# A network block on one core: the first stage rebuilt around row sums of squares, and four opening orders changed

## The chip, the cores and the metric

The kernel runs on one core of one Trainium2 chip. The metric is the device time of one execution in microseconds (us). Engines are named as the profile names them: PE (TensorE), DVE (VectorE), ACT (ScalarE), POOL (GpSimd) and SP (SyncE, which here only issues transfers).

## What is computed

All arrays are float32; the width D and the sequence are 1024, a context of 256 rows is read beside it. A block of two layers is followed by a pooling mixer and a convolutional FFN (hidden width 2816). Cut to what matters here:

```python
def rms_norm(x, g):
    y = x * lax.rsqrt(jnp.mean(x * x, axis=-1, keepdims=True) + EPS)
    return y * g

for i in range(2):
    shift, scale, gate = jnp.split(jax.nn.silu(c) @ ada_w[i] + ada_b[i], 3, axis=-1)   # and for c_ctx
    h = rms_norm(x, norm_g[i]) * (1.0 + scale) + shift
    if i == 0:
        lam = exp(sum(lambda_q1 * lambda_k1)) - exp(sum(lambda_q2 * lambda_k2)) + lam_init
        hc = rms_norm(ctx, norm_g[0]) * (1.0 + scale_c) + shift_c
        # proj = h @ w_in; k, v also of hc; differential attention with lam, a Fourier mix,
        # a silu gate, and the product with even_w_out
    else:
        bg, cg, xt, g = jnp.split(h @ odd_w_in, 4, axis=-1)
        u = cg * xt
        y = (bg * conv3(u, conv_w) * jax.nn.silu(g)) @ odd_w_out
    x = x + gate * y
x = x + pool_mixer(rms_norm(x, norm_mix_g))
val, gate = jnp.split(causal_conv3(rms_norm(x, norm_ffn_g) @ ffn_w_in, conv_w, conv_b), 2, axis=-1)
x = x + (jax.nn.silu(gate) * val) @ ffn_w_out
```

## The kernel before

The program is a row of blocks of code. In each block every engine runs its own list of instructions in the order in which it is written, and counters (semaphores) join them; nothing reorders. Most products are made in three passes of TensorE on operands that are split into a high and a low part (hi with hi, lo with hi, hi with lo): ACT makes the high part (`split_high`, L127), DVE or POOL the low part (`split_low`, L130). A tile has 128 partitions; D is eight tiles (`KT`), the sequence eight blocks of rows (`RT`), the context two (`CT`).

**First block**, `adaptive_parameters` (from L325). SP issues, in this order: the identity, x in two halves (2 MB each), 12 sets of small rows (biases, gains, the vectors c and c_ctx, taps) into `rows`, the four lambda vectors, the context (1 MB), and eight tiles of `ada_w` (1 MB each, `ada_raw`), then four slices of `even_w_in` (256 KB each). PE turns the small rows into columns (L388), turns x tile by tile into two pairs of PSUM banks (L398), makes ada products 0 to 2 (L299), turns the context (L416), and goes on with products 3 to 7, between which stand the column sums of the squares (L210, products with `ones`) and the spreads (L218, which turn a column of reciprocal roots into full rows). ACT copies each turned tile of x into `fq` (L447) and squares the tile before it (L154); DVE adds the squares up (L173). The context's squares are one instruction on ACT (L458) and one reduction on DVE (L488). Then come root, reciprocal, spread and the copies `rstd_x`, `rstd_c` (L183). When the last product is done, DVE copies its sum (`ada_rows`, L495), PE turns it (L307) and DVE makes shift and gain columns (L314, L320).

**Projections**, `even_projections` (from L560). For tile k of h, DVE multiplies x with gain and reciprocal root into `scaled` (L191, buffer `gate`), ACT adds the shift and rounds (`h_hi`, L165), DVE makes the rest (`h_lo`, L202). The class `Norm` holds these steps. PE (L685) starts tile k of the first unit (named k) when `h_lo` of tile k stands; a unit's slice of weights is split by ACT and POOL into `in_hi` and `in_lo`, in a ring of four.

**Conv stage**, `conv_layer` (from L1419) and **FFN**: both make products by a scheme of seven products for each group g, in the order p1, p6, p2, p5, p7, p3, p4 (`UP`). p1 and p2 use one bank, so p2 of group g waits for `p1_copy(g)` (L1758 in the conv stage, L2753 in the FFN) on ACT; p4 waits for c22, one of the sums that DVE makes out of finished banks (L1885, L2887). The first two groups are made without the scheme, and are copied out by `plain_out` (L1800, L2803). In the conv stage `gated_input` (DVE, L1908) makes u, `middle_tap` (ACT, L1768) the middle tap of the convolution, `tap_before` and `tap_after` (DVE, L1912, L1917) the others; `differences(kk)` (L1965) makes and splits operands of the seven products. In the FFN `ga_tap2` (ACT, L2780) and `ga_taps` (DVE, L2906, L2909) are the same for the gate half. N is the number of FFN groups; the products with `ffn_w_out` (L3090) follow in closing steps t, whose operands `high_pair` (ACT) and `low_s`, `low_t` (DVE, POOL) split into `down_ring`.

## Time and profile before

| | |
|---|---|
| median of 3 runs | 1856.58 us (1854.06 to 1858.5) |
| the profiled execution | 1857.68 us, its span 1855.9 us |
| mean granted TensorE clock | 0.985 of full |
| PE busy | 1774.3 us, 96% |
| DVE, ACT, POOL busy | 1167.8, 800.6, 757.2 us |
| moved by DMA | 188.31 MB, mean 101 GB/s |

A busy PE means that its matmuls follow each other, not that they run at full clock; the granted clock is listed apart, as a fraction of 2.4 GHz. Idle time of an engine that nobody waits for costs nothing. The time of one execution is its span and 1.8 us around it. The view of waits names for each wait what ended it; a bracket behind a row of the timeline says how long the engine had been idle before that row and who released it. A row of the timeline with a count stands for instructions that follow each other.

### The profile page before, as it was taken

The numbers are of one execution on the slowest core, as the hardware profiler recorded it, in microseconds if no ns is written. First come the engines' busy times: TensorE is split into PE (matmuls) and PEld (weight loads), VectorE is DVE, ScalarE is ACT, GpSimd is POOL, SyncE is SP. The second block draws the span as 40 slices with busy tenths as digits, with TensorE's granted clock in tenths as the row PEclk, the third lists the DMA queues.
The fourth block names the chain that finished last, engine by engine and source line by source line (L and its number), as shares of the span: only waits on it lengthen the run. The fifth ranks groups of instructions, "written<-read, shape, count | busy, mean of one in ns | idle before, by whom it ended". The sixth has DMA issues, their size and how long they took to land.

```text
span 1855.9 us, 22927 instructions
## 1 busy us (share of the span) xinstructions
PE 1774.3 (96%) x8745; PEld 1474.4 (79%) x8745; DVE 1167.8 (63%) x1315; ACT 800.6 (43%) x1244; POOL 757.2 (41%) x452
## 2 busy tenths in 40 slices
PE   5899999899999799999999999999999999999999
PEld 3688888668888688878888888987888888878887
DVE  3703876338888832965454653497666666779876
ACT  5324221346666632643333442655444444444443
POOL 0325322000000123356666531257999999920000
PEclk9899999899999999999999999999999999999999
DMA  8414113460000180212221341312232223187333
GB/s 324 149 48 117 46 46 102 177 245 1 0 0 0 46 268 32 65 57 79 69 80 57 118 155 46 94 43 73 76 91 80 91 80 91 57 310 262 138 120 124
DMA packets 162089, 188.31 MB, mean 101 GB/s; under 512 B 9231, under 2 KB 117320, under 8 KB 160840
## 3 DMA queue, kind: packets, MB, share of 16 engines
q1 hardware_dynamic: 161991, 187.00, 30.6%
q8 instruction: 64, 1.05, 0.2%
q14 instruction: 34, 0.27, 0.1%
HBM read 152.37 MB, written 34.60 MB: 101 GB/s over the span
## 4 chain that ended last, share of the span: by engine, by line
PE 50%; DVE 5%; ACT 2%; issue 2%; DMA 1%; POOL 0%; SPq 0%; ACTq 0%; DVEq 0%; POOLq 0%
PE ps L3039 18%; PE ps L2043 14%; PE ps L3090 10%; PE ps L2103 5%; PE ps L3390 1%; PE ps L3052 1%; DMA y_a<-y_scratch 1%; DVE cv_lo_p L130 1%; DVE up_lo_p L130 1%; DVE residual L2906 0%; DVE residual L1965 0%; ACT residual L3226 0%; DMA res_scratch<-x_nat 0%; PE ps L3056 0%; DVE residual L2945 0%
## 5 line engine op out<-in xcount | busy, mean ns | idle before, releaser
L3039 PE MATMUL ps<-up_hi_p,st_hi_p 128*128 128x512 f32 x560 | 218.0, 389 | 3.6 <-issue 2.0
L3039 PE MATMUL ps<-up_lo_p,st_hi_p 128*128 128x512 f32 x560 | 217.9, 389 | 0.0
L3039 PE MATMUL ps<-up_hi_p,st_lo_p 128*128 128x512 f32 x560 | 217.8, 389 | 0.0
L3090 PE MATMUL ps<-down_ring 128*128 128x512 f32 x924 | 210.7, 389 | 2.1 <-DVE down_ring L130 1.9
L3090 PEld LDWEIGHTS ps<-down_ring 128*128 128x128 f32 x924 | 173.2, 188 | 39.4 <-DVE down_ring L130 2.7
L130 POOL TENSOR_TENSOR in_lo<-in_raw,in_hi 128x512 fp32r<-128x512 f32 (+1 forms) x56 | 92.4, 1659 | 233.0 <-ACT in_hi L127 182.6
L2043 PE MATMUL ps<-cv_hi_p,cv_st_hi_p 128*128 128x512 f32 x392 | 153.4, 391 | 4.5 <-issue 4.5
L2043 PE MATMUL ps<-cv_lo_p,cv_st_hi_p 128*128 128x512 f32 x392 | 153.0, 390 | 0.0
L2043 PE MATMUL ps<-cv_hi_p,cv_st_lo_p 128*128 128x512 f32 x392 | 153.0, 390 | 0.0
L130 POOL TENSOR_TENSOR st_lo_p<-up_raw,st_hi_p 128x512 fp32r<-128x512 f32 x68 | 100.9, 1487 | 67.2 <-ACT st_hi_p L127 67.2
L3039 PEld LDWEIGHTS ps<-up_hi_p,st_hi_p 128*128 128x128 f32 x560 | 105.1, 188 | 26.2 <-issue 2.4
L1885 DVE TENSOR_TENSOR residual<-ps,residual 128x512 f32<-128x512 f32 x70 | 48.3, 691 | 120.4 <-PE ps L2043 120.4
L3039 PEld LDWEIGHTS ps<-up_hi_p,st_lo_p 128*128 128x128 f32 x560 | 105.1, 188 | 21.9
L3039 PEld LDWEIGHTS ps<-up_lo_p,st_hi_p 128*128 128x128 f32 x560 | 105.1, 188 | 21.6
L685 PE MATMUL ps<-in_hi,h_hi 128*128 128x512 f32 x256 | 100.8, 394 | 7.3 <-DVE h_lo L202 6.9
L1243 ACT ACTIVATE prob<-ps,neg_peak 128x1280 f32<-128x1280 f32 x64 | 84.9, 1327 | 48.2 <-DVE neg_peak L1337 48.2
L2887 DVE TENSOR_TENSOR residual<-ps,residual 128x512 f32<-128x512 f32 x100 | 68.0, 685 | 58.6 <-PE ps L3039 58.1
L1337 DVE TENSOR_REDUCE neg_peak<-ps 128x1 f32<-128x1280 f32 x64 | 95.2, 1487 | 11.4 <-PE ps L1149 11.3
L1149 PE MATMUL ps<-k_turned,q_turned 128*128 128x512 f32 (+1 forms) x384 | 91.7, 375 | 10.7 <-ACT prob L1243 4.6
L685 PE MATMUL ps<-in_lo,h_hi 128*128 128x512 f32 x256 | 100.6, 393 | 0.0
L685 PE MATMUL ps<-in_hi,h_lo 128*128 128x512 f32 x256 | 100.5, 392 | 0.0
L130 POOL TENSOR_TENSOR cv_st_lo_p<-cv_raw,cv_st_hi_p 128x512 fp32r<-128x512 f32 x50 | 74.7, 1502 | 52.1 <-ACT cv_st_hi_p L127 52.1
(377 smaller groups left out, 4209.0 us busy)
## 6 DMA issues: line engine op xcount, KB each, us to landing
up_raw<-in_ffn_w_in SPq DMA_DIRECT2D x44, 512.0 KB, 5.2
w_raw<-in_ffn_w_out SPq DMA_DIRECT2D x66, 256.0 KB, 3.0
ada_raw_rest<-in_ada_w SPq DMA_DIRECT2D x32, 512.0 KB, 6.1
cv_raw<-in_odd_w_in SPq DMA_DIRECT2D x32, 512.0 KB, 5.4
in_raw<-in_even_w_in SPq DMA_DIRECT2D x48, 256.0 KB, 2.8
y_scratch<-residual SPq DMA_DIRECT2D x22, 512.0 KB, 2.6
ada_raw<-in_ada_w SPq DMA_DIRECT2D x8, 1024.0 KB, 17.3
residual<-in_x SPq DMA_DIRECT2D x2, 2048.0 KB, 10.3
```

The source lines that it names most:

```text
L130: return eng.tensor_tensor(dst, src, high.bitcast(F32), ALU.subtract).then_inc(done, 1)
L685: last = pe.matmul(ps[:, bank, :], x[:, k, r * P:(r + 1) * P], w[:, n % RING, :], start=(k == 0 and x is x_hi and w is in_hi), stop=(k == ...
L1149: last = pe.matmul(score[m][:, b:e], q_turned[:, m, t * P:(t + 1) * P], k_turned[:, m, part, b:e], start=(part == 0), stop=(part == 1))
L1243: act.activation(prob[:, t % 2, m, :], score[m], ACT.Exp, bias=neg_peak[:, t, m:m + 1], accum_out=total[:, t, m:m + 1]).then_inc(sem("expe ...
L1337: dve.tensor_reduce(neg_peak[:, t, m:m + 1], score[m], AX_X, ALU.max, negate=True)\
L1885: dve.tensor_tensor(dst, ps[:, bank(g, p), :], base, ALU.add).then_inc(sem(name), 1)
L2043: last = pe.matmul(out, w[a_], x[b_], start=(first and a_ == 0 and b_ == 0), stop=(stop and a_ == 1), skip_group_check=skip)
L2103: last = pe.matmul(ps[:, 2 * (d % 4) + c, :], w[a_], x[k][:, c * BANK:(c + 1) * BANK], start=(k == 0 and a_ == 0 and x is y_hi), stop=(k = ...
L2887: dve.tensor_tensor(dst, ps[:, bank(j, p), :], base, ALU.add).then_inc(sem(name), 1)
L3039: last = pe.matmul(ps[:, bank(j, p), :], w[p][:, kk * P:(kk + 1) * P], x[p][:, kk, :], start=(first and w is st_hi and x is up_hi), stop=( ...
L3052: pe.matmul(ps[:, plain_bank(j, kind, side), :], part[FIRST_SLOT[j][kind, half]][:, ks], x_hi, start=(kk == 0 and half == 0 and part is st ...
L3090: last = pe.matmul(ps[:, 4 * (i % 2) + m, :], slot[:, s, m * P:(m + 1) * P], slot[:, x, :], start=(k == 0 and s == 0 and x == 2 and DOWN[i ...
```

## The change

Five things are edited.

1. The squares are summed along the natural rows of x and of the context: ACT squares a block of rows with a sum along the row into one column of `compact`. The squares of the turned tiles, their additions, the reduction of the context's squares and the products with `ones` are gone. DVE instead of ACT copies the turned tiles of x. PE spreads x's reciprocal roots behind ada product 1, the context's behind product 4.
2. The order of transfers: identity, x, the first 7 sets of small rows, ada 0 to 3, the context, ada 4 and 5, the other 6 sets, ada 6, weight slice 0, ada 7, slices 1 to 3. Column tile 0 is turned first, tiles 1 and 2 behind ada product 5. POOL splits slice 0 inside the first block.
3. Lambda is computed in the projections: its four loads stand behind the spills of x, its exponential on ACT ahead of the first root.
4. The first tile of h is made in halves of 512 columns; PE starts behind the left one. POOL waits for the first tile before it splits slices 1 to 3, and ACT's splits of these stand behind the first tile.
5. Four opening orders: conv stage, ACT `p1_copy(2)` behind `middle_tap(0)`; conv stage, DVE `gated_input(0)` behind `differences(3)`; FFN, ACT `ga_tap2(0)` ahead of `p1_copy(2)`; end of the FFN, ACT `ga_tap2(N - 1)` and `silu(N - 1)` each one `high_pair` earlier, DVE `ga_taps(N - 1)` ahead of `low_t(4)`, and `low_s(5)`, `low_t(5)` behind `product(N - 1)`.

```diff
--- the first block, transfers
-                        for t, r, src in row_sources:
+                        for t, r, src in row_sources[:FIRST_ROWS]:
                             sp.dma_start(rows[r:r + src.shape[0], t, :], src).then_inc(sem("rows_in"), 16)
-                        for n, name in enumerate(("even_lambda_q1", "even_lambda_k1", "even_lambda_q2", "even_lambda_k2")):
-                            sp.dma_start(lam_in[:, n, :], a[name].broadcast_to([P, DH])).then_inc(sem("lam_in"), 16)
-                        sp.dma_start(nat[:, RT:KEYT, :], ctx_rows).then_inc(sem("ctx_in"), 16)
                         for k in range(KT):
+                            if k == 4:
+                                sp.dma_start(nat[:, RT:KEYT, :], ctx_rows).then_inc(sem("ctx_in"), 16)
+                            if k == 6:
+                                for t, r, src in row_sources[FIRST_ROWS:]:
+                                    sp.dma_start(rows[r:r + src.shape[0], t, :], src).then_inc(sem("rows_late"), 16)
+                            if k == KT - 1:
+                                load_slice(sp, 0)
                             sp.dma_start(ada_raw[:, k, :], a["ada_w"][0, k * P:(k + 1) * P, 0:len(ADA_FIRST) * BANK])\
                               .then_inc(sem(f"ada_in{k}"), 16)
...
--- the first block, ACT
+                            act.activation(square[:, r % 2, :], nat[:, r, :], ACT.Square, accum_out=compact[:, r:r + 1])\
+                               .then_inc(sem(done), 1)
...
-                        for k in range(KT):
-                            act.wait_ge(sem("xt_turned"), k + 1)
-                            act.activation(x_t[:, k, :], pair[k % 2], ACT.Copy).then_inc(sem("xt_copied"), 1)
-                            if k:
-                                act.wait_ge(sem("xt_copied"), k)
-                                stats.scalar_square(act, k - 1)
+                        rooted(compact[:, 0:RT], "in_x_squared", RT, "in_x_rooted")
+                        act.wait_ge(sem("ctx_in"), 16)
+                        for r in range(RT, KEYT):
+                            squared(r, "c_squared")
+                        rooted(compact[:, RT:KEYT], "c_squared", CT, "c_rooted")
...
--- the first block, DVE
+                        for k in range(KT):
+                            dve.wait_ge(sem("xt_turned"), k + 1)
+                            dve.tensor_copy(x_t[:, k, :], pair[k % 2]).then_inc(sem("xt_copied"), 1)
...
--- the projections, first tile on DVE
+            def vector_first_halves(self, dve):
+
+                self.scale(dve, 0, LEFT, "scaled_left")
+                self.scale(dve, 0, RIGHT, "scaled")
+                dve.wait_ge(self.s("high_left"), 1)
+                self.lower(dve, 0, LEFT, "low_left")
+                dve.wait_ge(self.s("high"), 1)
+                self.lower(dve, 0, RIGHT, "low")
...
--- the projections, ACT
-                        for n in range(1, RING):
-                            high_slice(act, n)
                         for k in range(KT):
-                            norm_x.scalar_high(act, k)
+                            if k == 0:
+                                norm_x.scalar_high_left(act)
+                            norm_x.scalar_high(act, k, RIGHT if k == 0 else None)
+                            if k == 0:
+                                for n in range(1, RING):
+                                    high_slice(act, n)
...
--- the conv stage, ACT
-                p1_copy(2)
                 for kind, side in PLAIN_OUT:
                     plain_out(1, kind, side)
                 for p in ("p3", "p4"):
                     high_stationary(act, p, 2)
-                moving_stands(act, "p4", HALF - 1)
                 middle_tap(0)
                 for g in range(2, G - 1):
-                    if g > 2:
-                        p1_copy(g)
+                    p1_copy(g)
...
--- the conv stage, DVE
+                differences(3)
                 gated_input(0)
-                differences(3)
...
--- the FFN, ACT
+                ga_tap2(0)
                 p1_copy(2)
-                ga_tap2(0)
...
--- the end of the FFN, DVE
+                ga_taps(N - 1)
                 low_t(dve, SLOTS)
-                low_s(dve, LOW_FIRST)
-                low_t(dve, LOW_FIRST)
-                ga_taps(N - 1)
                 product(N - 1)
```

The first block on PE before, from the turns of the small rows (L388) to the turn of the last sum (L307); L299 is an ada product, L210 a sum of squares, L218 a spread, L416 a turn of the context:

```order
1 L388 MATMUL ps<-ident,rows 128x120
2 L388 MATMUL ps<-ident,rows 128x104
3 L388 MATMUL ps<-ident,rows 128x89
4 L398 MATMUL ps<-ident,residual 128x128 x64
5 L299 MATMUL ps<-ada_raw,cond 32x512 x12
6 L416 MATMUL ps<-ident,residual 128x128 x16
7 L299 MATMUL ps<-ada_raw,cond 32x512 x12
8 L210 MATMUL ps<-ones,square_sum 128x1 x8
9 L299 MATMUL ps<-ada_raw,cond 32x512 x4
10 L210 MATMUL ps<-ones,square_sum_c 128x1 x2
11 L218 MATMUL ps<-ident,compact 128x128 x8
12 L299 MATMUL ps<-ada_raw,cond 32x512 x4
```

The same place on PE now (L283 is the ada product, L374 a spread, L405 a turn of the context):

```order
1 L367 MATMUL ps<-ident,rows 128x120
2 L393 MATMUL ps<-ident,residual 128x128 x64
3 L283 MATMUL ps<-ada_raw,cond 32x512 x8
4 L374 MATMUL ps<-ident,compact 128x128 x8
5 L283 MATMUL ps<-ada_raw,cond 32x512 x8
6 L405 MATMUL ps<-ident,residual 128x128 x16
7 L283 MATMUL ps<-ada_raw,cond 32x512 x4
8 L374 MATMUL ps<-ident,compact 128x128 x2
9 L283 MATMUL ps<-ada_raw,cond 32x512 x4
10 L367 MATMUL ps<-ident,rows 128x104
11 L367 MATMUL ps<-ident,rows 128x89
12 L283 MATMUL ps<-ada_raw,cond 32x512 x8
```

The sums with `ones` are gone, both spreads stand ahead of product 5, and the context's turns moved from behind product 2 to behind product 3.

The opening of the conv stage on ACT before; L1758 is `p1_copy(2)`, L1800 `plain_out(1)`, L1768 `middle_tap(0)`, L1776 `silu`, L1762 the copy of c11:

```order
275 L1758 ACTIVATE residual<-ps 128x512
276 L1800 ACTIVATE residual<-ps 128x512 x4
277 L127 ACTIVATE cv_st_hi_p<-cv_odd_sums 128x512
278 L127 ACTIVATE cv_st_hi_p<-cv_raw 128x512
279 L1768 ACTIVATE residual<-residual,cols 128x1024
280 L127 ACTIVATE cv_st_hi_p<-cv_raw 128x512
```

And now (L1818 `plain_out(1)`, L1786 `middle_tap(0)`, L1776 `p1_copy(2)`):

```order
265 L1818 ACTIVATE residual<-ps 128x512 x4
266 L128 ACTIVATE cv_st_hi_p<-cv_odd_sums 128x512
267 L128 ACTIVATE cv_st_hi_p<-cv_raw 128x512
268 L1786 ACTIVATE residual<-residual,cols 128x1024
269 L1776 ACTIVATE residual<-ps 128x512
270 L128 ACTIVATE cv_st_hi_p<-cv_raw 128x512
```

The copy that p2 of group 2 waits for moved from ahead of seven instructions to behind them.

## Rows read from the trace of the kernel before

**Rows 1.** The page, part 1: busy time, share and instructions of PE.

```profile
PE 1774.3 (96%) x8745; PEld 1474.4 (79%) x8745; DVE 1167.8 (63%) x1315; ACT 800.6 (43%) x1244; POOL 757.2 (41%) x452
```

**Rows 2.** PE's waits from 12 to 60 us: total us, times, longest.

```profile
PE ps L388 <- DMA rows<-in_even_subln: 16.8, 1, 16.8
```

**Rows 3.** Busy time by stretch: start:end, length, PE, PEld, DVE, ACT, POOL, clock, DMA, GB/s.

```profile
14.40:18.10 3.70, 1.32 (x7) 1.33 (x8) 0.50 (x3) 0.00 (x0) 0.00 (x0) 1.00 0.16 40
22.00:32.00 10.00, 6.93 (x60) 4.87 (x62) 4.90 (x4) 10.00 (x12) 0.00 (x0) 1.00 1.01 424
```

**Rows 4.** The tile ada_raw: its eight loads' issues, and issue to landing.

```profile
L378 SPq DMA_DIRECT2D ada_raw<-in_ada_w x8: 432/600/3479, 11.1 to 18.4; - x8
...
DMA to landing us min/median/max: 13.0/17.3/24.0
```

**Rows 5.** Timeline, first block: start, us, engine, line, operation; bracket: idle before, releaser.

```profile
24.83 1.03 ACT L447 ACTIVATE fq<-ps 128x1024 f32<-128x1024 f32 x1
25.73 1.07 ACT L154 ACTIVATE gate<-fq 128x1024 f32<-128x1024 f32 x1
...
46.50 1.07 PE L299 MATMUL ps<-ada_raw,cond 128*32 128x512 f32 x8
...
46.60 1.78 DVE L183 COPY residual<-ps 128x1024 f32<-128x1024 f32 x2 [0.47 <-PE ps L218]
48.30 0.68 DVE L495 COPY ada_rows<-ps 128x512 f32<-128x512 f32 x1
```

**Rows 6.** Timeline, start of the projections.

```profile
50.72 3.49 DVE L191 SCALAR_TENSOR_TENSOR gate<-fq,mod_gain,residual 128x1024 f32<-128x1024 f32 x2 [0.32 <-PEq L366]
50.77 9.01 POOL L130 TENSOR_TENSOR in_lo<-in_raw,in_hi 128x512 fp32r<-128x512 f32 x4 [50.32 <-POOLq L366]
...
54.13 2.29 DVE L202 SCALAR_TENSOR_TENSOR h_lo<-gate,ada_col,h_hi 128x1024 fp32r<-128x1024 f32 x1
...
56.57 0.76 PE L685 MATMUL ps<-in_hi,h_hi 128*128 128x512 f32 x1 [6.87 <-DVE h_lo L202]
...
62.10 1.28 DVE L202 SCALAR_TENSOR_TENSOR h_lo<-gate,ada_col,h_hi 128x1024 fp32r<-128x1024 f32 x1
```

**Rows 7.** Stretches with a granted clock of 0.50; columns as in rows 3.

```profile
37.78:41.20 3.42, 3.42 (x17) 0.78 (x21) 1.92 (x2) 3.40 (x3) 0.00 (x0) 0.50 0.99 405
51.40:61.70 10.30, 5.13 (x12) 4.09 (x13) 10.23 (x6) 4.28 (x5) 8.38 (x4) 0.50 0.32 94
809.20:812.60 3.40, 3.17 (x8) 2.53 (x9) 0.72 (x2) 0.29 (x1) 3.40 (x4) 0.50 0.38 154
```

**Rows 8.** Timeline by engine, opening of the conv stage (DVE, ACT, PE).

```profile
788.57 2.31 DVE L1908 TENSOR_TENSOR residual<-residual 128x1024 f32<-128x1024 f32 x1
...
797.74 2.12 DVE L1912 SCALAR_TENSOR_TENSOR residual<-residual,cols 128x1023 f32<-128x1023 f32 x1 [3.66 <-ACT residual L1768]
...
793.10 0.58 ACT L1758 ACTIVATE residual<-ps 128x512 f32<-128x512 f32 x1
...
796.53 1.18 ACT L1768 ACTIVATE residual<-residual,cols 128x1024 f32<-128x1024 f32 x1
...
793.88 0.41 PE L2043 MATMUL ps<-cv_hi_p,cv_st_hi_p 128*128 128x512 f32 x1
...
809.42 0.77 PE L2043 MATMUL ps<-cv_hi_p,cv_st_hi_p 128*128 128x512 f32 x1 [4.48 <-issue]
```

**Rows 9.** Timeline by engine, opening of the FFN (ACT, PE).

```profile
1261.83 1.25 ACT L2780 ACTIVATE residual<-residual,cols 128x1024 f32<-128x1024 f32 x1 [3.06 <-DVE up_lo_p L130]
...
1273.62 0.47 PE L3039 MATMUL ps<-up_hi_p,st_hi_p 128*128 128x512 f32 x1 [2.05 <-issue]
...
1283.56 0.47 PE L3039 MATMUL ps<-up_hi_p,st_hi_p 128*128 128x512 f32 x1 [1.53 <-ACT residual L2753]
```

**Rows 10.** Timeline of DVE, closing products of the FFN.

```profile
1649.96 1.27 DVE L2906 SCALAR_TENSOR_TENSOR residual<-residual,cols 128x1023 f32<-128x1023 f32 x1
...
1664.78 0.69 DVE L2565 TENSOR_TENSOR y_a<-y_a 128x512 f32<-128x512 f32 x1 [1.45 <-DMA y_a<-y_scratch]
```

More of the change, by code:

```diff
@@ L199, in vector_scale @@
                             dve.wait_ge(self.s("low"), k)
-                        scale(k + 1)
+                        self.scale(dve, k + 1, whole, "scaled")
                     dve.wait_ge(self.s("high"), k + 1)
-                    dve.scalar_tensor_tensor(out=self.low(k), in0=self.scaled[:, k % 2, 0:self.n], scalar=self.shift(k),
-                                             in1=self.high(k).bitcast(F32), op0=ALU.add, op1=ALU.subtract)\
-                       .then_inc(self.s("low"), 1)
-            def tensor_mean(self, pe, sums):
-                pe.wait_ge(self.s("summed"), sums)
-                for r in range(self.n // P):
-                    last = pe.matmul(self.mean[:, r:r + 1], self.total[:, r * P:(r + 1) * P], ones[:, 0:1],
-                                     start=True, stop=True)
-                last.then_inc(self.s("meaned"), 1)
+                    self.lower(dve, k, whole, "low")
             def tensor_spread(self, pe, parts=1):
@@ L401, in _ @@
                         pe.wait_ge(sem("cond_ready"), 1)
-                        def ada(first, end):
-                            for k in range(first, end):
-                                pe.wait_ge(sem(f"ada_in{k}"), 16)
-                                last = ada_product(pe, ADA_FIRST, 6, k, cond,
-                                                   [ada_raw[:, k, i * BANK:(i + 1) * BANK] for i in range(len(ADA_FIRST))])
-                            return last
-                        ada(0, 3)
+                        ada(0, 2)
+                        spread(spread_x, range(RT), "in_x_inverse").then_inc(sem("in_x_spread"), 1)
+                        ada(2, 4)
                         pe.wait_ge(sem("ctx_in"), 16)
+                        pe.wait_ge(sem("xt_copied"), KT)
                         for k in range(0, KT, 4):
@@ L671, in _ @@
                     def _(pool):
-                        for n in range(N_SLICES):
+                        pool.wait_ge(norm_x.s("low"), 1)
+                        for n in range(1, N_SLICES):
                             pool.wait_ge(sem("in_high"), n + 1)
```

224 lines of the change are left out of this document (116 added, 108 removed).

## The prediction

> **What bounds the kernel now.** I read the page first: TensorE (PE) is busy 96% of the span [rows 1], so only time in which PE stands, or runs at a low clock, can be won. Its waits come next: 16.8 us for the first loads, in the stage that the change rebuilds [rows 2]. Then the transfers: the share of the DMA engines and the GB/s say whether a stretch is bound by loading. They run full, 424 GB/s, through the middle of the first block, but from 14.4 to 18.1, where only small rows and the lambda vectors are under way, they are nearly idle [rows 3]. The last tile of `ada_raw` is issued at 18.4 and lands 24.0 us later, at 42.4 [rows 4]. The timeline of the first block shows the rest: a copy on ScalarE (ACT) with a square behind it for each turned tile of x, and after the last ada product (46.50) a row of short dependent steps [rows 5]. The projections' start is a chain on VectorE (DVE) from 50.72 to PE's 56.57, with 6.87 us of waiting on PE [rows 6]. Of TensorE's clock, three stretches show a granted 0.50, that is 1.2 instead of 2.4 GHz [rows 7]. Last, the openings of the conv stage, of the FFN and of its closing products, where PE or DVE wait 4.48, 2.05, 1.53 and 1.45 us [rows 8 to 10].
>
> **First block, from its start to E.** Call E the moment at which the projections may begin (50.72, the first DVE scale [rows 6]). Loads first. Before, the 2.48 us that one MB of `ada_raw` takes at 424 GB/s [rows 3] are paid for 4 MB of x, 1 MB of ctx and 8 MB of ada; between the end of x (14.4) and the return of the full rate (18.1) lie 3.7 us in which mostly the 16 small loads are under way [rows 3], and by the sizes of their arrays they carry some 0.3 MB. The change leaves 7 of them ahead, puts 6 behind ada5 (between large ones, which can keep the engines full), moves four (lambda) out of the block and brings slice 0 (256 KB, 0.62 us) in. If the small loads behind large ones are nearly free, the last ada tile lands about 2.1 us earlier for them (9 of 16 small loads' share of 3.7) and 0.62 later for the slice: 42.4 - 2.1 + 0.6 = 40.9.
>
> The TensorE side: x turns start when 7 instead of 12 rows have come, about 15.7 instead of 16.8. Before, each tile took a period of 1.86, which is ACT's copy of 1.03 and its square of 1.07 less overlap (24.83 and 25.73 are the starts of one pair, 0.9 apart [rows 5]). After, DVE copies alone; 128x1024 plus 128x256 took 1.78 in two copies [rows 5], so 1.2 to 1.4 for one, and eight take some 11 us instead of 15, to about 28. ACT takes the sums from natural rows meanwhile (10 squares of about 1.07, 10.7 us, starting as soon as the first half of x lies), so it is no bound. Gone from DVE are seven additions and one reduction, from PE ten small matmuls. Then PE follows the ada tiles: the last product begins at 41.1 if the clock is high, and at 43.1 if it falls at about 37 as it did at 37.78 for 3.42 us [rows 7], since an ada product of 1.07 (the eight matmuls at 46.50 [rows 5]) then takes 2.1. Before, it began at 46.50, 4.1 us after its data, because ctx copies, sums and spreads stood ahead of it in PE's order.
>
> From that product to E took 50.72 - 46.50 = 4.22, of which 0.7 were the wait of the `ada_rows` copy (48.30) for the two rstd copies (46.60 to 48.38) on DVE [rows 5]; those now lie earlier. That leaves 3.5, so E is 44.6 to 46.7; since the block still has pauses of the kind that preceded the low clock, I take 45.9: **-4.8** (bounds -3.8 and -6.0).
>
> **From E to the first matmul.** Before: two whole scales, 3.49 for the pair beside GpSimd (POOL), `h_hi` 1.1, `h_lo` 2.29, and PE starts at 56.57, E + 5.85 [rows 6]. After: the left half's scale, high, low. The price of a whole `h_lo` alone is 1.28 (at 62.10) against 2.29 while POOL works [rows 6], and POOL now waits for the first tile's low. Half of 1.28 is 0.68 with the fixed part; two halves of the scale queue before the low on DVE, ACT's half high (0.6) lies beside the second. 0.68 + 0.6 + 0.7 + some 0.2 of signals = 2.2: **-3.65** (bounds -3.0 and -4.0). What is late next? Tile 1: POOL's three splits, moved behind the first low, meet its scale, and ACT splits slices 1 to 3 (3 x 0.6) first. Its low ends at about E + 9.3; PE is through tile 0 at the low clock at E + 2.2 + 7.1 to 8.8, that is E + 9.3 to 11. No stall, with little to spare. Lambda moves into the projections, where PE has work and DVE's steps go ahead of a norm that waits for PE anyway; its result is wanted only in the attention. Without that cover its nine tiny instructions would cost under 3 us. Stage sum: **-8.45**.
>
> **Conv opening.** PE's p2(2) must wait for `p1_copy(2)` (the ACT row L1758 at 793.10 [rows 8]), which goes behind the first middle tap (L1768). The tap waits for `gated_input(0)` (DVE L1908, 2.31 at 788.57), now behind `differences(3)`. Before, p2(2) began at 793.88 [rows 8]; after, DVE makes the differences first, ACT is done with its splits and plain outputs some 1.5 us sooner, the tap starts at about 795 to 796 and the copy is done at 796.5 to 797: a new stall of 2.7 to 3.1 at p2(2). It lies under the old one: PE stood 4.48 us, until p4(2) at 809.42, because c22 came late on DVE behind the two taps that began at 797.74 [rows 8]. The taps now begin 1.0 to 1.6 us sooner, so p4(2) starts at 807.8 to 808.5: -0.9 to -1.6. The 3.40 us of low clock behind that stop [rows 7] cost 1.7. One long pause becomes a shorter one and almost none; either the clock stays (-1.7 more), or it falls at p2 and costs the same there under cover. I take **-2.0** (bounds -0.3, if the fall delays p4(2) too, and -3.0).
>
> **FFN opening.** `p1_copy(2)` goes behind `ga_tap2(0)` (L2780), which waits to 1261.83 [rows 9]. PE's four products p2, p5, p7, p3 took 809.42 - 4.48 - 793.88 = 11.06 in the conv stage [rows 8]; the same before 1273.62 - 2.05 puts p2(2) of the FFN at 1260.5. Now it starts at 1261.83 + 1.15 + 0.6 + 0.1 = 1263.7, a stall of 3.2. The pause of 2.05 before 1273.62 takes 2.05 of it, so p4(2) is 1.1 late; the pause of 1.53 before 1283.56, which waits for ACT's next copy, takes part of that. **+0.7** (0 to +2.0, the upper end with a fall of the clock).
>
> **FFN closing.** On DVE `ga_taps(N-1)` (L2906 and its twin, two of 1.27 from 1649.96 [rows 10]) moves ahead of `low_t(4)`, for which PE waits: 2.0 to 3.0 of new stall. The 1.45 for which DVE waits for a landing before 1664.78 [rows 10] may take part of it, though that load is issued later too: **+1.75** (0.9 to 2.6).
>
> **Sum.** -4.8 - 3.65 - 2.0 + 0.7 + 1.75 = -8.0. Against the profiled execution (1857.68, span 1855.9) that is 1849.7; the median of the runs (1856.58) lies 1.1 lower, by which it is 1848.6. I take **1849.0**.
>
> **The rivals.**
> Small loads cost the same wherever they stand. For it: 3.7 us for 16 of them at 32 GB/s [rows 3]. Then only the lambda loads are saved, the last tile lands at about 42.2, and with a low clock E is 47.7: 1.8 less, 1850.8.
> The Trainium skill, DMA: Bandwidth & Descriptors, section Rules for kernel authors, says of many small transfers to coalesce them, since under 64 KB one pays mostly overhead; moving them would not help by that. No row here shows small ones between large ones, so the trace does not decide it; by the rule the sum would be the 1850.8 of this rival.
> The orders cost more than said: conv gains nothing (0 for -2.0) and the FFN's clock falls (+2.0 for +0.7): -4.7, 1852.3.
> The clock stays high at the projections' start. It was low for 10.30 us from 51.40 [rows 7], behind PE's long idle; a pause of 2.2 instead of 5.9 may not bring it down: 2.5 to 3 more, 1846.2. Against it: the fall at 37.78 [rows 7] came behind much shorter pauses than the one before 56.57.
> The block is not shorter, since something unseen replaces its chain, and only the halves help: -3.2, 1853.8.
> **The slower side.** The low clock at the start lasts on. A tile is 24 matmuls, two of the products of 2.76 worked out above: 5.5 at the high clock, 11 at half of it. DVE makes a tile's operands in 4.4 us beside POOL (2 x 2.2 [rows 6]), and now PE is 3.65 us nearer to them. If PE runs into `h_lo` of tiles 1, 2, 3 and the clock therefore stays low through three tiles more, that is 3 x 5.5 less 2 that it costs already, +14, so +6 against before: 1863. It decides from where tile 1's `h_lo` comes later than the end of tile 0, at E + 9.3 to 11.
>
> **How the numbers follow.** Forecast 0.53, small loads 0.15, orders 0.12, clock high 0.12, block not shorter 0.05, slower 0.03. A measurement of this kernel tells about 0.2% (3.7 us) from no change, so faster means below 1852.9: nearly all of the forecast, of the small loads and of the high clock, and half of the orders, 0.85; the same 0.11; slower 0.04. The bounds of the terms add (as independent) to about 2.5 either way; with the high clock at 1846 and the orders at 1852.3 the range is 1845.0 to 1853.5.
>
> **What would show it.** After: the last ada product at 41 to 43.5 and E at 44.6 to 46.7; first projection matmul at E + 2.2; no PE wait at tile 1; a wait of about 3 before p2(2) in the conv stage, and at most a short one before p4(2), with p4(2) of the same products then 0.9 to 1.6 us nearer to the stage's start; a wait of 3.2 at p2(2) of the FFN and of 2 to 3 at its fourth closing step. I am wrong if the DMA rate sinks where the six rows stand, if PE waits for `h_lo` of tile 1, or if the stalls at p2(2) reappear in full at p4(2).

## The result

The changed kernel takes 1844.70 us (median of 6 runs, 1842.64 to 1848.65) where the kernel before takes 1855.62 (6 runs, 1854.04 to 1858.5). The ratio is 0.9942, with a 95% interval of 0.9929 to 0.9954: 10.9 us, or 0.6%, faster. The forecast was 1849.0 with a range of 1845.0 to 1853.5. The direction was right, and three of the five terms came out within their bounds. The first block gained more than its bounds allowed and the closing products lost less; the whole gain was larger than the range allowed, by 0.3 us.

The two profiled executions have spans of 1855.9 and 1846.2, so the traces have 9.7 us to explain. First the page of the changed kernel, its busy times and clock.

```profile
span 1846.2 us, 22891 instructions
PE 1773.9 (96%) x8725; PEld 1474.8 (80%) x8725; DVE 1167.8 (63%) x1317; ACT 798.6 (43%) x1250; POOL 762.2 (41%) x452
```

PE does the same work as in [rows 1], to 0.4 us. What went is time in which it stood. Its waits in the changed kernel, total us, times, longest:

```profile
PE ps L367 <- DMA rows<-in_c_ctx: 15.9, 1, 15.9
...
PE ps L3101 <- DVE down_ring L131: 3.7, 2, 2.1
PE ps L689 <- DVE h_lo L172: 3.5, 1, 3.5
...
PE ps L3050 <- ACT residual L2768: 2.9, 1, 2.9
...
PE ps L2058 <- ACT residual L1776: 2.7, 1, 2.7
```

The first row answers [rows 2] (16.8). The wait for `h_lo` is 3.5 where [rows 6] has 6.87. The waits of 4.48 and 2.05 at p4(2) (p4 of group 2) [rows 8, 9] are gone, and in their place stand 2.7 and 2.9 at p2(2), for `p1_copy(2)`, as the prediction said; the closing products wait 3.7 instead of 1.9.

The transfers, in the stretches of [rows 3] (length, PE, PEld, DVE, ACT, POOL, clock, DMA share, GB/s) and where they end:

```profile
14.40:18.10 3.70, 2.16 (x10) 2.16 (x11) 0.28 (x1) 3.65 (x7) 0.00 (x0) 1.00 0.99 394
22.00:32.00 10.00, 9.58 (x79) 5.67 (x78) 7.19 (x8) 2.69 (x6) 0.00 (x0) 1.00 1.03 411
...
39.00:40.00 1.00, 1.00 (x14) 0.24 (x8) 0.00 (x0) 0.00 (x0) 0.00 (x0) 0.85 0.56 209
40.00:41.00 1.00, 1.00 (x13) 0.38 (x16) 0.43 (x2) 0.00 (x0) 0.00 (x0) 1.00 0.05 18
```

The pause behind x, 40 GB/s before, is gone altogether: 394 GB/s. That is the row that the prediction had not foreseen. The last tile of `ada_raw` is issued at 21.99 and lands at 39.13, where the kernel before had 42.47 and the prediction 40.9. The timeline of the first block and of the projections' start:

```profile
35.70 1.80 PE L283 MATMUL ps<-ada_raw,cond 128*32 128x512 f32 x8 [1.11 <-ACT residual L450]
...
39.96 1.92 PE L283 MATMUL ps<-ada_raw,cond 128*32 128x512 f32 x16
...
44.38 1.41 DVE L168 SCALAR_TENSOR_TENSOR gate<-fq,mod_gain,residual 128x512 f32<-128x512 f32 x2 [0.32 <-PEq L341]
45.92 1.41 DVE L172 SCALAR_TENSOR_TENSOR h_lo<-gate,ada_col,h_hi 128x512 fp32r<-128x512 f32 x2
...
46.81 0.77 PE L689 MATMUL ps<-in_hi,h_hi 128*128 128x512 f32 x1 [3.46 <-DVE h_lo L172]
```

E, the first DVE scale, is at 44.38 (50.72 in [rows 6]), and PE starts the projections at 46.81, 2.43 behind it (5.85 before). The low clock, as in [rows 7]:

```profile
35.90:39.30 3.40, 3.40 (x18) 0.49 (x10) 0.42 (x1) 0.63 (x1) 1.27 (x1) 0.50 0.97 381
46.10:52.90 6.80, 6.08 (x14) 4.81 (x15) 6.80 (x5) 4.31 (x6) 5.49 (x3) 0.50 0.17 52
786.80:790.20 3.40, 3.40 (x10) 2.62 (x9) 3.37 (x3) 0.02 (x1) 2.19 (x2) 0.50 0.53 157
1251.00:1254.40 3.40, 3.10 (x7) 2.49 (x8) 2.34 (x3) 3.38 (x7) 1.67 (x1) 0.51 0.00 0
```

It now falls at p2(2) in both schemes (PE starts these at 786.44 and 1251.30). In the conv stage it is no longer at p4(2); in the FFN the first trace of before had none at the opening.

### The profile page after: what moved, and what is told of

The parts are those of the page before. It is cut to its first block, busy times and chain, and to the rows that moved or that the text cites. A ratio compares the mean times of both kernels' runs of the same rounds, so it can differ in the third digit from the quotient of the medians.

```text
span 1846.2 us, 22891 instructions
## 1 busy us (share of the span) xinstructions
PE 1773.9 (96%) x8725; PEld 1474.8 (80%) x8725; DVE 1167.8 (63%) x1317; ACT 798.6 (43%) x1250; POOL 762.2 (41%) x452
## 4 chain that ended last, share of the span: by engine, by line
PE 52%; DVE 4%; ACT 2%; issue 1%; DMA 1%; SPq 0%; ACTq 0%; DVEq 0%
PE ps L3050 20%; PE ps L2058 14%; PE ps L3101 10%; PE ps L2118 5%; PE ps L3401 1%; PE ps L3063 1%; DMA y_a<-y_scratch 1%; DVE cv_lo_p L131 1%; DVE up_lo_p L131 1%; DVE residual L1980 0%; ACT residual L3237 0%; PE ps L3067 0%; DVE residual L2959 0%; ACT cv_hi_p L128 0%; ACT residual L1797 0%
## 5 line engine op out<-in xcount | busy, mean ns | idle before, releaser
L131 POOL TENSOR_TENSOR in_lo<-in_raw,in_hi 128x512 fp32r<-128x512 f32 (+1 forms) x56 | 97.7, 1754 | 218.4 <-ACT in_hi L128 172.4
L1169 PE MATMUL ps<-k_turned,q_turned 128*128 128x512 f32 (+1 forms) x384 | 91.7, 375 | 10.6 <-ACT prob L1263 4.5
## 6 DMA issues: line engine op xcount, KB each, us to landing
residual<-in_x SPq DMA_DIRECT2D x2, 2048.0 KB, 10.4
```

The lines of the kernel that those rows point to most:

```text
L131: return eng.tensor_tensor(dst, src, high.bitcast(F32), ALU.subtract).then_inc(done, 1)
L1169: last = pe.matmul(score[m][:, b:e], q_turned[:, m, t * P:(t + 1) * P], k_turned[:, m, part, b:e], start=(part == 0), stop=(part == 1))
```

## Where the 9.7 us come from, and how much of it is chance

From the first projection matmul on, PE runs the same matmuls in the same order in every kernel here. So the start of one and the same matmul can be compared between two traces, and the lead of one kernel over the other be read at each place. The table has the lead over the first trace of the kernel before, in us, where that trace stands at the time in the head. It has all traces, those of the experiments too (the part that differs is named in the section of each).

| kernel | 56.57 | 330 | 370 | 790 | 812.9 | 1255 | 1500 | end |
|---|---|---|---|---|---|---|---|---|
| changed | 9.76 | 9.27 | 11.09 | 10.32 | 11.96 | 12.30 | 11.74 | 9.70 |
| changed, second trace | 10.63 | 10.56 | 13.30 | 13.65 | 14.07 | 15.55 | 15.71 | 13.97 |
| e1 old orders | 10.04 | 11.49 | 14.56 | 13.88 | 13.49 | 14.48 | 14.73 | 14.66 |
| e2 old closing | 10.46 | 11.68 | 14.77 | 14.13 | 15.85 | 16.23 | 15.57 | 15.15 |
| e3 conv order only | 10.56 | 10.59 | 13.29 | 13.68 | 14.03 | 15.47 | 15.75 | 15.34 |
| e10, the same kernel | 9.86 | 11.31 | 14.38 | 13.88 | 15.64 | 16.01 | 16.26 | 15.43 |
| e5 small rows ahead | 9.70 | 10.15 | 10.38 | 9.77 | 12.91 | 13.29 | 12.76 | 13.18 |
| e6 lambda loads ahead | 6.73 | 6.27 | 8.10 | 7.43 | 9.16 | 9.56 | 8.89 | 8.00 |
| e7 first tile whole | 9.14 | 9.63 | 9.61 | 10.03 | 11.94 | 14.76 | 13.96 | 12.86 |
| e11 context in two pairs | 11.26 | 12.34 | 15.29 | 10.49 | 12.18 | 15.17 | 15.38 | 14.70 |
| before, second trace | 0.02 | 0.24 | 0.66 | 0.84 | 0.95 | 3.44 | 3.50 | 2.80 |
| e4 orders alone | 0.16 | 1.08 | 1.36 | 2.63 | 4.32 | 4.37 | 2.34 | 1.00 |
| e9 lambda moved alone | 0.96 | 1.46 | 1.24 | 1.88 | 1.83 | 1.84 | 2.06 | 0.91 |

Two traces of the same program differ by 2.8 (before) and by 4.3 us (changed) at the end, and they part where nothing was edited and where the low clock fell at another place. So a term is read from its own stretch, as a mean over the traces that have the edit less those that don't. Behind each mean stands an estimate of its 95% interval from the scatter of these traces:

- first stage, at 330: the six traces with the whole new stage have 10.8, the three with the old one (both of before and e4) 0.4: **-10.4** (1.2 either way)
- conv opening, 790 to 812.9: ten traces with the new order gain 1.6, four with the old one lose 0.1: **-1.7** (0.6)
- FFN opening, 1255 to 1500: seven new ones lose 0.7, seven old ones gain 0.2: **+0.9** (0.6)
- closing products, 1500 to the end: six new ones lose 1.1, eight old ones 0.5: **+0.6** (0.9, so not clear of nothing)

The sum is -10.6, beside -10.9 and (second timing, below) -9.5 between medians. It leaves out the stretches 330 to 790 and 812.9 to 1255, where nothing was edited. In them the ten traces with a new first stage gain 2.5 us on the mean and the four with the old one 1.3; between 345 and 370 it is 2.1 against 0.1, and elsewhere part of that is lost again. Whether this difference of 1.3 belongs to the change stays open (below), so the close agreement of the sum with the medians is in part luck.

## Experiments

### e6 and e5: which small loads made the pause?

e6 puts four loads of the lambda vectors back to their old place, into a tile that is not read:

```diff
+                        for n, name in enumerate(("even_lambda_q1", "even_lambda_k1", "even_lambda_q2", "even_lambda_k2")):
+                            sp.dma_start(lam_first[:, n, :], a[name].broadcast_to([P, DH])).then_inc(sem("lam_first"), 16)
                         for k in range(KT):
                             if k == 4:
```

> The changed kernel with four more loads of the lambda vectors, into a tile that nobody reads, behind the first 7 small sets and ahead of ada 0, where the old kernel had them. Theory A (these broadcast loads made the pause of 3.7 us): a stretch of 2.5 us or more with under 100 GB/s comes back behind x, the DMA engines are done 2.5 or more later (42 or later), and E is 1 to 2.5 later than 44.4. Theory B (their share of 16 small loads): 0.9 later, E at most 0.5 later.

e5 puts all the sets of small rows ahead and leaves lambda where it is:

```diff
-                FIRST_ROWS = 7
+                FIRST_ROWS = len(row_sources)
```

> The changed kernel with all 12 sets of small rows loaded ahead of the ada tiles, as before; lambda's loads stay in the projections. In the changed kernel the 3.7 us in which the DMA engines were nearly idle are gone altogether, though 7 small sets still stand ahead. Theory A (that pause was made by the four lambda loads): the rate stays near 400 GB/s from 14 to 18 us, PE starts 0.9 later (16.8), the DMA engines are done within 0.5 of the changed kernel's 39.6 and E (first DVE scale) within 0.6 of 44.4. Theory B (each small load costs its share, 0.23): five more ahead bring a pause of 1.2 behind x and E is about 45 to 46.

(The kernel has 13 sets of small rows, not the 12 named so far: 7 ahead and 6 behind.)

The stretch of the pause, first of e6, then of e5:

```profile
14.40:18.10 3.70, 1.93 (x9) 1.94 (x10) 0.28 (x1) 3.22 (x7) 0.00 (x0) 1.00 0.17 52
```

```profile
14.40:18.10 3.70, 0.93 (x5) 0.93 (x6) 0.28 (x1) 3.44 (x7) 0.00 (x0) 1.00 1.00 371
```

With lambda's loads the pause is back: 52 GB/s, a DMA share of 0.17. With all small rows ahead and no lambda there is none. The end of the first block in e6 (PE, then DVE):

```profile
43.56 1.06 PE L283 MATMUL ps<-ada_raw,cond 128*32 128x512 f32 x8 [2.11 <-DMA ada_raw<-in_ada_w]
...
47.40 1.42 DVE L168 SCALAR_TENSOR_TENSOR gate<-fq,mod_gain,residual 128x512 f32<-128x512 f32 x2 [0.32 <-PEq L342]
```

PE now waits for the last ada tile, which lands at 43.52 instead of 39.13, and E is 47.40, 3.0 later than in the changed kernel. The expectation had 1 to 2.5; the landing moved by 4.4 us, more than the pause of 3.7 that it reckoned with. The one run of e6 took 1849.65 us, that of e5 1844.46, beside 1858.48 of the kernel before.

E of e5 is 44.43, within 0.05 of the changed kernel's first trace. That does not make the place of the rows worth nothing, for the clock differs between the two. E of e5, then of the changed kernel's second trace:

```profile
44.43 1.42 DVE L168 SCALAR_TENSOR_TENSOR gate<-fq,mod_gain,residual 128x512 f32<-128x512 f32 x2 [0.32 <-PEq L341]
```

```profile
43.50 1.42 DVE L168 SCALAR_TENSOR_TENSOR gate<-fq,mod_gain,residual 128x512 f32<-128x512 f32 x2 [0.32 <-PEq L341]
```

The table sorts the traces by the clock beneath ada product 4 (times in us):

| traces | low clock | last tile lands | product 4 starts | last product starts | E |
|---|---|---|---|---|---|
| changed, e1, e10 | from 35.8 to 36.0, for 3.4 | 38.9 to 39.1 | 35.4 to 35.7 | 40.6 to 40.8 | 44.1 to 44.4 |
| changed (second), e2, e3 | none there | 39.1 to 39.2 | 36.4 to 36.6 | 40.0 to 40.1 | 43.5 to 43.7 |
| e5 small rows ahead | none there | 39.60 | 37.35 | 40.91 | 44.43 |
| e6 lambda loads ahead | none there | 43.52 | 36.93 | 43.56 | 47.40 |

At the same clock e5 is 0.9 later than the changed stage and e6 3.8. In e5 PE starts at 17.17 instead of 15.9, because it waits for the last of 13 sets instead of 7, and from product 4 on it takes the same 3.56 us. So the four lambda loads made the pause. The six sets of rows moved the last landing by 0.4 and made no pause, but their place is worth 0.9 through PE's start.

The table shows a second thing. Where the clock is low beneath product 4, PE had been 0.9 ahead there: in the changed kernel's first trace its turns of x start every 0.21 us until 18.8 and every 0.11 behind that, in the second trace this comes at 21.1. The low clock then costs 1.6 between product 4 and the last one (5.14 against 3.56), and E is 0.7 later in the end.

What makes the lambda loads slow is not shown. They differ from the rows in two ways at once: they write 128 partitions, and in pieces of 256 bytes. In the stretch of the pause 445 of 461 packets of the kernel before were under 512 bytes, 368 of 386 in e6, and 17 of 193 in e5.

### e9: lambda moved, nothing else

The kernel before, with lambda's four loads and its arithmetic taken out of `adaptive_parameters` and put into `even_projections` as the change does:

```diff
-                        for n, name in enumerate(("even_lambda_q1", "even_lambda_k1", "even_lambda_q2", "even_lambda_k2")):
-                            sp.dma_start(lam_in[:, n, :], a[name].broadcast_to([P, DH])).then_inc(sem("lam_in"), 16)
...
-                        act.wait_ge(sem("lam_dots"), 2)
-                        act.activation(lam_exp[:, :], lam_dot[:, :], ACT.Exp).then_inc(sem("lam_exped"), 1)
```

> The kernel before with one part of the change: lambda's loads and arithmetic moved into the projections; sums, tile copies, halves and orders as before. So far: E (first whole DVE scale) 50.72 before, 47.40 with the new sums and lambda's loads ahead, 44.38 with both. Theory A (loads and the chain of sums are two limits, one behind the other): the pause of 3.7 us goes and the ada tiles land 3.7 earlier, but PE's last ada product stays behind the sums and ACT's copies; these start 1.2 us earlier (ACT no longer waits for lambda's sums before its first copy), so E is 49.3 to 49.8 and the kernel 1 to 1.5 us faster than before. Theory B (the loads were the only limit): E about 47, the kernel 3.7 us faster.

Measured: 1856.94 against 1855.47, ratio 1.0006 (0.9994 to 1.0018): nothing that can be told. The trace shows why (the pause's stretch, the last ada product on PE, E on DVE):

```profile
14.40:18.10 3.70, 1.35 (x7) 1.35 (x8) 0.53 (x3) 0.00 (x0) 0.00 (x0) 1.00 1.02 374
```

```profile
45.55 1.06 PE L299 MATMUL ps<-ada_raw,cond 128*32 128x512 f32 x8
...
49.76 3.50 DVE L191 SCALAR_TENSOR_TENSOR gate<-fq,mod_gain,residual 128x1024 f32<-128x1024 f32 x2 [0.32 <-PEq L362]
```

The pause is gone and the last tile lands at 38.49 instead of 42.47, but the last product starts only 0.95 earlier, since sums and spreads stand ahead of it on PE, and E is 49.76. Theory A had 49.3 to 49.8 for E; the 1 to 1.5 us that it gave the kernel lie below what the timing can show (the interval allows 1.1 at most). With e6 this makes a table of two parts by two, E in us ("new sums and copies" stands for the whole new first block but lambda; the changed kernel has 44.38 with the low clock beneath product 4 and 43.5 to 43.7 without, as e6 has it):

| | lambda's loads ahead | lambda in the projections |
|---|---|---|
| old sums and copies | 50.72 | 49.76 |
| new sums and copies | 47.40 | 44.38 |

Lambda's move alone is worth 1.0, the new sums and copies alone 3.3, and both together 6.3: two chains that end nearly together. 2.1 us belong to the pair alone (2.9 at e6's clock).

### e7: the first tile of h whole

```diff
-                        norm_x.vector_first_halves(dve)
+                        norm_x.scale(dve, 0, slice(0, SEQ), "scaled")
+                        dve.wait_ge(norm_x.s("high"), 1)
+                        norm_x.lower(dve, 0, slice(0, SEQ), "low")
                         norm_x.vector_scale(dve, 1)
```

with ACT's high part and PE's wait for the whole tile to match.

> The changed kernel with the first tile of h made whole; POOL still waits for it, and ACT's splits of slices 1 to 3 stay behind it. Theory A (halves and the quiet POOL each carry a part): scale 1.28, high 1.15, low 1.28 and signals, first matmul at E + 3.9 against E + 2.4 in halves, so 1.5 of the 3.4 are the halves and 1.9 are the order of POOL and ACT. Theory B (the halves carry it all): E + 5.5 or more.

DVE, then PE:

```profile
43.50 1.28 DVE L168 SCALAR_TENSOR_TENSOR gate<-fq,mod_gain,residual 128x1024 f32<-128x1024 f32 x1 [0.32 <-PEq L341]
46.00 1.28 DVE L172 SCALAR_TENSOR_TENSOR h_lo<-gate,ada_col,h_hi 128x1024 fp32r<-128x1024 f32 x1 [1.22 <-ACT h_hi L155]
...
47.43 0.77 PE L687 MATMUL ps<-in_hi,h_hi 128*128 128x512 f32 x1 [4.95 <-DVE h_lo L172]
```

The first matmul is at E + 3.93, against E + 2.43 in halves and E + 5.85 before. Theory A: 1.5 of the 3.4 us are the halves, 1.9 are the order (one tile ahead of the slices on ACT, POOL quiet, 1.28 for an operation instead of 2.29 as in [rows 6]). No run separates ACT's part of the 1.9 from POOL's. E is 43.50 here, as in the traces of the changed stage with no low clock beneath product 4; the one run took 1844.78 us.

### e1, e4: the opening orders on the two first stages

e1 is the changed kernel with all four orders as before; e4 is the kernel before with all four orders new. Their diffs are the last parts of the diff of the change, undone and done.

> The changed kernel with all four opening orders as before; only the first stage is new. Theory A (the terms are separate and add, as the two profiles read): the first projection matmul stays 9.8 us earlier than before, the conv opening gives its 1.8 us back, the FFN opening and the closing products save 0.7 and 1.95; so 0.85 us faster than the changed kernel, about 11 us under the kernel before (ratio 0.994). Rival B (the orders matter more than read, since the low clock behind the conv stall moves with them): 2 to 3 us slower than the changed kernel. Rival C (the 1.8 us that the changed kernel gained at 346 to 368 us, where nothing was edited, is a matter of the clock in one execution): the profile shows the gain there as anything between 0 and 2.

> The kernel before with the four new opening orders and the old first stage. Theory A: +0.7 and +1.95 against -1.8, so 0.85 us slower than before, ratio 1.0005; in the profile p2 of group 2 of the conv stage waits 2.7, p4 about 0.3, and the FFN's p2 3.1. Rival B: 2 to 3 us faster than before. Where the first stage's shift decides the conv stage's clock, the stretch of low clock lies elsewhere than in the changed kernel.

Measured: e1 1846.13 us, ratio 0.9954 (0.9936 to 0.9971); e4 1854.37, ratio 0.9991 (0.9979 to 1.0004). Rival B, that the orders bring 2 to 3 us, is not excluded by these intervals alone; theory A fits e1, and for e4 its 1.0005 lies just outside. The traces decide. PE's waits in e4, 700 to 1300, and in e1, 700 to 850:

```profile
PE ps L3032 <- ACT residual L2750: 3.0, 1, 3.0
PE ps L2040 <- ACT residual L1758: 2.7, 1, 2.7
```

```profile
PE ps L2061 <- issue: 4.4, 1, 4.4
```

e1 keeps the stop of 4.4 at p4(2) whatever the first stage is; e4 has the two stops at p2(2). In the table, e4 gains 1.69 over the conv opening and loses 2.03 over the FFN's and 1.34 at the end; e1 loses 0.4, gains 0.25 and loses 0.07. In the long mean they make -1.7 + 0.9 + 0.6 = -0.2, known to about 1.2 either way: four edits that nearly cancel, and rival B's 2 to 3 us are not there. Rival C of e1 is taken up with the second trace of before, below: between 345 and 370 the lead grew by 3.07 in e1, more than the 0 to 2 it named, and by 0.28 in e4.

### e2, e3, e10 and a second run of the changed kernel: the two orders that cost

e2 has the closing order as before, e3 that and the FFN's opening order; e10 is e3 once more, timed beside the changed kernel on one chip. The FFN's edit and the closing's main edit:

```diff
-                ga_tap2(0)
                 p1_copy(2)
+                ga_tap2(0)
...
-                ga_taps(N - 1)
                 low_t(dve, SLOTS)
+                low_s(dve, LOW_FIRST)
+                low_t(dve, LOW_FIRST)
+                ga_taps(N - 1)
                 product(N - 1)
```

> The changed kernel with only the closing order as before. Theory A: the wait of 2.1 before the fourth closing step goes, the waits of 1.0 before two later steps return, net 1.95 us faster than the changed kernel (ratio to before 0.9931). Rival (the 2.1 are taken back at the step that waits for a landing): 0.8 or less.

> The changed kernel with the FFN's opening order and the closing order as before; the conv order stays new. Theory A: 0.7 + 1.95 = 2.65 us faster than the changed kernel, 13.5 under the kernel before (ratio 0.9927). Rival: the stalls that these two orders make are taken back by the pauses behind them, and nothing changes (ratio 0.994).

> The changed kernel with the FFN's opening order and the closing order as before, timed beside the changed kernel itself on one chip. From the traces so far: these two new orders cost 0.9 us (1255 to 1500) and 0.7 (1500 to the end) on the mean of the executions, so this kernel should be 1.6 us under the changed one, ratio to before 0.993. Rival: no difference (0.994).

> The changed kernel once more, timed beside the one with only the conv order, and for a second trace of it. Expected: ratio to before 0.994; the first projection matmul 9.7 to 10.6 us earlier than before; in the stretch 345 to 370, where one trace of it gained 1.8, anything from 0 to 3 by where the low clock falls.

Measured: e2 1843.78, ratio 0.9941 (0.9922 to 0.9961); e3 1843.11, 0.9935 (0.9916 to 0.9955); e10 1842.03, 0.9927 (0.9914 to 0.9939); the changed kernel again 1846.00, 0.9947 (0.9935 to 0.9960). The kernel with only the conv order is 4.0 us under the changed kernel where both were timed side by side, and 1.6 where they were timed apart (e3 and the first result); the traces give 1.5 (0.9 + 0.6). The intervals of e10 and of the changed kernel overlap by 0.0004, so the sign is well supported and the size is not. e2 alone is not told apart from the changed kernel.

The closing stall itself, in the changed kernel:

```profile
1641.38 0.93 PE L3101 MATMUL ps<-down_ring 128*128 128x512 f32 x3 [2.10 <-DVE down_ring L131]
```

It costs 2.1 where it stands (11.74 at 1500, 9.40 just behind it), and part comes back over the next steps, which waited before as well. In e5 the stall was 1.16 and all of it came back (12.76 at 1500, 13.18 at the end). That is the rival of e2, and it is nearer to the mean of 0.6 than theory A's 1.95.

### The kernel before once more: is the gain at 345 to 370 the change's?

> The kernel before once more, for a second trace of it. In the stretch from 345 to 370 us, where nothing was edited, four kernels with the new first stage were 1.8 to 3.1 us faster than the one trace of before, and the new orders on the old first stage 0.3. Theory A (this is where the low clock happens to fall in an execution, and has nothing to do with the change): this trace differs from the first one of before there by 1 us or more, one way or in the clock's place. Theory B (the new first stage does it): the same within 0.4.

The lead there is 0.42, with the low clock at 345.0 and 355.2 in place of 351.8 (the one run took 1854.85 us). That decides nothing: it is just beyond theory B's 0.4, short of theory A's 1 us, and the clock's place did change, as A has it. The other traces tell more. Two kernels with the new first stage, e5 and e7, have 0.20 and -0.05, and eight have 1.8 to 3.1; the four with the old stage have -0.2 to 0.4. The lead goes with how long the clock was low around these turns of k and q:

| low clock there, us | traces | lead gained, 345 to 370 |
|---|---|---|
| 3.4 or 6.8 | changed (second), e1, e2, e3, e10, e11 | 2.7 to 3.1 |
| 10.2 in two parts | changed, e6 | 1.8 |
| 10.2 in one part | before, e4 | 0 and 0.3 |
| 13.7 in two parts | before (second), e5, e7, e9 | -0.2 to 0.4 |

So the gain there goes with the length and the place of the low clock. Why that is shorter in most kernels with the new stage, and not in e5 and e7, stays open; with it stays open whether the change has a part in these 2 us.

### e11: the context in two pairs of banks

e3's kernel, and in the first block:

```diff
-                                    last = pe.transpose(pair[0][:, (i * CT + r) * P:(i * CT + r + 1) * P],
+                                    last = pe.transpose(pair[k // 4][:, (i * CT + r) * P:(i * CT + r + 1) * P],
...
                             last.then_inc(sem("ct_turned"), 1)
-                            pe.wait_ge(sem("ct_copied"), k // 4 + 1)
                         ada(4, 5)
+                        pe.wait_ge(sem("ct_copied"), 2)
```

> The changed kernel with the FFN's opening and the closing order as before, and one thing new: the two turns of the context go into two pairs of PSUM banks, and PE goes on with ada product 4 without waiting for ACT's copies. In the changed kernel PE stood 1.11 before and 1.11 behind the second turn, and the low clock from 35.9 followed. Theory A (after lambda's loads are gone, PE's chain and the loads end nearly together; the DMA engines are done at 39.5): PE reaches product 4 at about 33.5 instead of 35.7, then follows the landings; the last product starts at 39.8 to 40.3 instead of 40.9, E at 43.2 to 43.7 instead of 44.4, 0.7 to 1.2 us earlier than in the changed kernel; the whole 1 us under the kernel with only the conv order, ratio to before 0.992. Theory B (PE's pauses there were covered by waiting for ada tiles anyway): E within 0.3 of 43.5 to 44.4, as the changed kernels had it with either clock.

```profile
39.31 1.07 PE L283 MATMUL ps<-ada_raw,cond 128*32 128x512 f32 x8 [1.17 <-DMA ada_raw<-in_ada_w]
...
42.87 1.42 DVE L168 SCALAR_TENSOR_TENSOR gate<-fq,mod_gain,residual 128x512 f32<-128x512 f32 x2 [0.32 <-PEq L341]
```

E is 42.87, the earliest of all, and the last product waits for its tile (landed at 39.27): from here the first block is bound by its loads. Against the traces with the same clock (43.5 to 43.7) that is 0.7 earlier. The lead at the first projection matmul is 11.26 against 9.76 to 10.63. No low clock falls before 40 us, but that is so in three of the six traces of the unedited stage too. The time, 1842.94 us, ratio 0.9928 (0.9902 to 0.9954), tells it neither from e10 nor from the changed kernel.

## Why the prediction came out as it did

**The first block, -4.8, was the term that failed.** Its mean over the traces of the changed stage is 6.8 (E at 43.5 to 44.4). The step was "the last ada tile lands about 2.1 us earlier for them (9 of 16 small loads' share of 3.7)". The pause was not shared out among the small loads; four of them, lambda's, made all of it (e6, e5). So the last tile landed at 39.1 and not at 40.9. From there PE did not follow the ada tiles either, as the prediction had it: its own chain, with the context's turns and copies in it, put the last product at 40.0 to 40.8, and e11 shows that the loads would have allowed 39.3. The share was miscounted as well: there are 17 small loads, and 6 rows and 4 lambda loads make 10 of them (2.2 us, so nothing hangs on it). The rows could have warned: the pause had a DMA share of 0.16 [rows 3], but no row separates the loads there.

**The choice within that term** was the second fault, and as large: I took 45.9 between 44.6 and 46.7, with a fall of the clock. The low clock came in three of six traces of the changed stage. It cost 1.6 where it stood, not 2.0, and E was 0.7 later with it. Of the 2.0 us by which the term was too small, 1.0 is the high-clock bound (44.6 against 43.6 measured) and 1.0 is this choice.

**E to the first matmul, -3.65,** was right: -3.42; e7 splits it into 1.5 for the halves and 1.9 for the order. Tile 1 did not stall. Lambda in the projections cost nothing that shows: the leads at 56.57 and at 330 differ by less than the clock moves them.

**Conv opening, -2.0:** -1.7, so the size was right. The new stall of 2.7 came (2.7 to 3.1 said), the old stop of 4.48 went, and DVE's taps began 1.6 sooner (1.0 to 1.6 said; 785.84 with a lead of 10.32). But p4(2) was to start 0.9 to 1.6 us nearer to the stage's start, and it hardly moved. The row is the changed kernel's p4(2):

```profile
799.05 0.39 PE L2058 MATMUL ps<-cv_hi_p,cv_st_hi_p 128*128 128x512 f32 x1
```

Against 809.42 [rows 8] that is a lead of 10.37, where it was 10.32 ahead of the stall. PE did not wait there, since it reached p4(2) only then: the low clock at p2(2) had made it 1.6 later. The fall was not under cover, which was the condition of the small bound of -0.3. What saved the term is that the low clock of 3.40 us behind p4(2) was gone; it stands at p2(2) instead. In e5, where the clock did not fall at p2(2), p4(2) came 1.7 nearer.

**FFN opening, +0.7:** +0.9, stall 2.9 to 3.0 (3.2 said).

**Closing, +1.75,** was mis-sized: +0.6, below its bound of 0.9, though the scatter reaches up to it. The stall of 2.1 came (2.0 to 3.0 said); what was given back behind it was taken for too little.

**The base.** The forecast of 1849.0 is 8.0 under 1857.0, between the profiled execution and a median of three runs; six runs gave 1855.62. So of the 4.3 us by which it was too high, 1.4 are the base and 2.4 the terms. That the range was missed by 0.3 is chance: the interval of the ratio leaves 1842.4 to 1847.1, and the second timing of the changed kernel, 1846.00, lies within the range. That the first block was 2 us better than said is not chance.

**The rivals.** Small loads the same wherever they stand: it was right that only the lambda loads are saved, and wrong in their price, a share by count; the last tile landed at 39.1 and not at 42.2. Beside it stood the rule of the Trainium skill, DMA: Bandwidth & Descriptors, section Rules for kernel authors, to coalesce small transfers, since under 64 KB one pays mostly overhead. For the rows the trace agrees in small part: six sets of at most 44 KB, ahead instead of behind, moved the last landing by 0.4 us and PE's start by 1.2, with the engines full (371 GB/s, e5). No run loads them as one. Orders cost more than said: no. Clock high at the projections' start: in part. It was low from 46.1 for 6.8 us in the changed kernel, and for 3.4 in e1, e2, e10 and e11; before it was 10.2. In these four the lead grew by 1.1 to 1.5 up to 330, in the traces with 6.8 it moved by -0.5 to 0.5. Block not shorter: no. The slower side, operands of tiles 1 to 3 late: no wait of PE there.

## What to carry over

Where a stretch of loading is nearly idle, find out which load makes it before pricing it by count: put one kind back alone. Two chains that end together, loads and the work behind them, hide each other: shortened alone they brought 1.0 and 3.3 here, and both together 6.3. Test by two and two. Before two traces are compared for an edit of 1 us, look whether the clock was low at the same places in both; e5 seemed to change nothing and changed 0.9. And where one run differs from the next by more than an edit is worth, compare the start of the same instruction between traces, stretch by stretch, over several traces.

## What the runs showed of the hardware

- Four loads that each spread one row of 64 floats over 128 partitions (32 KB written) took about 3.7 us of the queue that all large loads share: 40 and 52 GB/s with them, 394, 371 and 374 without, while up to 13 loads of 0.5 to 44 KB in rows of 512 bytes left no such pause.
- Between executions of one program the low clock fell at other places, and PE's lead moved with it: 2.8 us between two traces of before, 4.3 between two of the changed kernel. With the stops of 2.6 to 3.0 us at p2(2) the granted clock fell to 0.50 in 15 of 17 cases (at 786.8 and 1251.0 in the changed kernel), for 3.4 or 6.8 us, in some of them while PE still stood.
- A square with its sum along the row on ACT was followed by a read of the accumulator of 0.19 us: 1.04 us between blocks of 128x1024.
